# Loading expert matrices whole, 2 MB in seven buffers, instead of in halves in fourteen

## Chip, core and metric

The kernel runs on one core of one Trainium2 chip. The metric is device time in microseconds for one execution. A core has TensorE (PE, with its weight loads as PEld), VectorE (DVE), ScalarE (ACT), GpSimd (POOL) and SyncE (SP), and 16 DMA engines that carry out the transfers that SP, ACT and POOL issue.

## What is computed

One decoder layer on 512 tokens of width 1024, in float32. A combined projection feeds two attention branches, their gated outputs are merged and added to `x`, then comes a mixture of experts with 4 groups of 8, then a gated per-layer embedding and a final norm. The expert part, cut to what matters:

```python
D_MODEL = 1024; SEQ = 512; N_EXPERTS = 32; EXPERT_TOPK = 2; D_EXPERT = 512
expert_id = g[:, None] * EXPERTS_PER_GROUP + top_idx      # two experts of one group per token
def block_fn(args):                                       # for the rows of one expert
    tok_b, e_b = args
    xb = h_pad[tok_b]
    hid = jax.nn.silu(jnp.matmul(xb, w_gate[e_b])) * jnp.matmul(xb, w_up[e_b])
    return jnp.matmul(hid, w_down[e_b])
# w_gate, w_up: (32, 1024, 512); w_down: (32, 512, 1024); every matrix is 2 MB of float32
```

The weighted results are added back to the token rows.

## The kernel before

The program is written out by hand for each engine, with semaphores between them. Up to the routing (the front) its weights come in halves of 8 KB per partition into the ring `raw`, are split by ACT and DVE into two parts `w_hi` and `w_lo`, and multiplied. When the attention is done, ACT writes the normed rows to `h2_rows` in DRAM (profile name `h_rows`, line 1130), POOL gathers for each expert up to 64 of its rows into `xg` (three buffers, line 1545), PE turns them (line 854) and DVE scales them into `xt`.

The expert loop goes over 32 experts. `gate_up(e)` multiplies the rows by gate and up, eight k-tiles of 128 rows each (lines 878 and 879, side by side in the two halves of the array's columns; the trace shows two matmuls for each in the code); ACT and DVE make the hidden rows of it (lines 1143 and 1471); PE turns them (line 859, into `ht`, line 1487), and `down(e)` multiplies them, four k-tiles (lines 894 and 895). ACT weighs the result into `y` (line 1149), and POOL scatters it to `pair_rows` in DRAM (line 1550). PE's order is `gate_up(e + 1)`, the turn of the rows of `e + 2`, the turn of the hidden rows of `e`, `down(e)`.

All expert weights come through SP's queue (line 579), in the order of their use: `EXPERT_HALVES` lists gate and up of expert 0, then for each e gate and up of `e + 1` and down of `e`, every matrix cut into two halves: 128 partitions with 8 KB in a row, taken from rows that are 16 KB long in DRAM. A half holds four of the eight k-tiles of gate or up, or two of the four of down. There are 192 halves and fourteen buffers of 1 MB (`SLOTS`), which lie over memory of the front that comes free: `qk` when the branch products are done, the four `raw` buffers one by one as the splits (`lo_done`) go on, `w_hi`, `w_lo` and half of `act_hi` after the last `out` product, and one over `act_lo` after `h2_rows` is written (`h2_out`). From the fifteenth load on, SP waits for `half_used`, which PE raises when it is done with a half:

```python
        for n, (what, e, h) in enumerate(EXPERT_HALVES):
            if n >= SLOTS:
                sp.wait_ge(half_used, n - SLOTS + 1)
```

PE waits for each half by the semaphore of its buffer (`slot_loaded`). SP waits in order: a load whose wait isn't met holds back all behind it. Behind the experts stand six loads of the tail (`tail_raw`, line 532: two of `ple_proj` with 512 KB, four of `ple_gate` with 1 MB), also into expert buffers (`TAIL_RAW`), each behind the last use of its buffer, and then the loads of the summed pairs `y_in_even` and `y_in_odd` (line 600), which wait for the last scatter. A branch for experts with more than 64 rows (`over`) has loads of its own at line 591; the trace holds none of them.

Of the kernel before, what the change touches and what calls it, by code (L numbers as in the profile page):

```python
# [8 lines left out]
F32 = mybir.dt.float32  # L9
# [26 lines left out]
AHEAD = 2  # L36
SLOTS = 14
FIRST = 64
# [184 lines left out]

EXPERT_HALVES = expert_halves()
PLACE = {h: n for n, h in enumerate(EXPERT_HALVES)}
N_EXP = len(EXPERT_HALVES)
SLOT_REGION = [("qk", 0), ("qk", 1)] + [("raw", (N_FRONT - RAW + k) % RAW) for k in range(RAW)]
SLOT_REGION += [("whi", k) for k in range(SPLIT)] + [("wlo", k) for k in range(SPLIT)] + [("hi", 0), ("lo", 0)]
assert len(SLOT_REGION) == SLOTS
# [3 lines left out]
OVER_SLOTS = TAIL_HI + TAIL_LO  # L233
assert N_TAIL == 6 and N_EXP % SLOTS == 10

# [9 lines left out]
def layer_kernel(nc, x, p, g_attn, w_in, w_br_a, w_br_b, w_out, g_ffn, w_grp, b_grp, w_rt, b_rt,  # L245
# [13 lines left out]
    def sb(name, region, shape, dt=F32, skip=0):  # L259
        return nc.alloc_sbuf_tensor_at(name, shape, dt, offset=start[region] + skip)  # L260
# [10 lines left out]
    def sem(name):  # L271
# [6 lines left out]

    slot = [sb(f"slot_{k}", r, [P, HALF_W], skip=8 * K * j) for k, (r, j) in enumerate(SLOT_REGION)]
    slot_at = lambda k: start[SLOT_REGION[k][0]] + 8 * K * SLOT_REGION[k][1]  # L280
    tail_raw = [nc.alloc_sbuf_tensor_at(f"tail_raw_{m}", [P, HALF_W // (2 if m < 2 else 1)], F32, offset=slot_at(k) + skip)
                for m, (k, skip) in enumerate(TAIL_RAW)]
    tail_hi, tail_lo = ([nc.alloc_sbuf_tensor_at(f"tail_{n}_{j}", [P, HALF_W], F32R, offset=slot_at(k))
                         for j, k in enumerate(at)] for n, at in (("hi", TAIL_HI), ("lo", TAIL_LO)))
    raw_at = [raw[:, n % RAW, :] for n in range(N_FRONT)] + [v[:] for v in tail_raw]
# [29 lines left out]
    y_over = sb("y_over", "stage", [P, D], skip=4 * K)[:]  # L315
    xt = sb("xt", "hi", [P, 2, KD, FIRST], skip=8 * K)[:]
    xt_over = sb("xt_over", "hi", [P, KD, P], skip=12 * K)[:]
    ht = sb("ht", "lo", [P, FE // P, FIRST], skip=8 * K)[:]
    ht_over = sb("ht_over", "lo", [P, FE // P, P], skip=10 * K)[:]
    y_in = [nc.alloc_sbuf_tensor_at("y_in_even", [P, 2 * D], F32, offset=slot_at(Y_SLOT))[:],  # L320
            sb("y_in_odd", "small", [P, 2 * D])[:]]
# [155 lines left out]
    def split_high(act, n):  # L477
        if n < N_FRONT:
            act.wait_ge(raw_loaded[n % RAW], 16 * (n // RAW + 1))
            if n >= SPLIT:  # L480
                act.wait_ge(half_started, n - SPLIT + 2)
        else:
            m = n - N_FRONT
            act.wait_ge(tail_loaded[m], 16)
            if m < SPLIT:
                act.wait_ge(half_used, max(last_in_slot(TAIL_HI[m]), last_in_slot(TAIL_LO[m])) + 1)
# [11 lines left out]
    def split_next(s):  # L498
        n = HALF_OF[s] + AHEAD
        return n if n < (N_FRONT if HALF_OF[s] < N_FRONT else N_FRONT + N_TAIL) else None  # L500

    OVER_HALVES = [(what, h) for what in ("gate", "up", "down") for h in range(2)]
# [15 lines left out]
    def _(sp):  # L518
# [42 lines left out]

        def half_source(what, e, h):
            return views[what][e][:, h * HALF_W:(h + 1) * HALF_W]

        for n, (what, e, h) in enumerate(EXPERT_HALVES):
            if n >= SLOTS:
                sp.wait_ge(half_used, n - SLOTS + 1)
            elif SLOT_REGION[n][0] == "qk":
                for t in range(NT):
                    filled(sp, ("branch_b", 1, "tile", t))  # L570
            elif SLOT_REGION[n][0] == "raw":
                sp.wait_ge(lo_done, N_FRONT - RAW + n - 2 + 1)
            elif SLOT_REGION[n][0] in ("whi", "wlo"):
                filled(sp, ("out", 1, "tile", NT - 1))
            elif SLOT_REGION[n][0] == "hi":
# [8 lines left out]
        with sp.If(n_over > 0):  # L584
            with sp.Fori(0, NOVER) as i:
                with sp.If(i < n_over):
                    sp.wait_ge(half_used, N_EXP)
                    code = sp.value_load(over[0:1, bass.ds(i, 1)], min_val=0, max_val=NE * CH - 1)
                    e = sp.snap(code // CH, min_val=0, max_val=NE - 1)
                    for r, (what, h) in enumerate(OVER_HALVES):  # L590
                        sp.dma_start(slot[OVER_SLOTS[r]][:], half_source(what, e, h)).then_inc(ov_loaded[r], 16)
# [17 lines left out]
    def _(pe):  # L609
# [251 lines left out]

        def weights(slot_n, k):
            return slot[slot_n][:].rearrange("p (k n) -> p k n", k=k)

        def loaded(e, what, h):
            n = PLACE[what, e, h]
            pe.wait_ge(slot_loaded[n % SLOTS], 16 * (n // SLOTS + 1))
            return n % SLOTS

        def gate_up(e):  # L870
            ps = bank[2 + e % 2]
            pe.wait_ge(xt_done, e + 1)
            for h in range(2):
                g, u = (weights(loaded(e, what, h), 4) for what in ("gate", "up"))
                for k in range(4):
                    left = xt[:, e % 2, 4 * h + k, :]
                    first, last = h == 0 and k == 0, h == 1 and k == 3
                    mm_g = pe.matmul(ps[FIRST:2 * FIRST, :], left, g[:, k, :], start=first, stop=last)  # L878
                    mm_u = pe.matmul(ps[0:FIRST, :], left, u[:, k, :], start=first, stop=last)  # L879
                mm_g.then_inc(half_used, 1)  # L880
                mm_u.then_inc(half_used, 1)
            pe.sem_inc(pe_steps, 1)
            return mm_u

        def down(e):
            ps = bank[5 + e % 2]
            if e >= 2:
                pe.wait_ge(y_done, e - 1)
            for h in range(2):
                w = weights(loaded(e, "down", h), 2)  # L890
                for k in range(2):
                    first, last = h == 0 and k == 0, h == 1 and k == 1
                    left = ht[:, 2 * h + k, :]
                    pe.matmul(ps[0:FIRST, :], left, w[:, k, 0:512], start=first, stop=last)  # L894
                    mm = pe.matmul(ps[FIRST:2 * FIRST, :], left, w[:, k, 512:1024], start=first, stop=last)  # L895
                mm.then_inc(half_used, 1)

# [22 lines left out]
        with pe.If(n_over > 0):  # L920
            with pe.Fori(0, NOVER) as i:
                with pe.If(i < n_over):
# [4 lines left out]
                    for r, (what, h) in enumerate(OVER_HALVES[0:4]):  # L927
                        pe.wait_ge(ov_loaded[r], 16 * i + 16)
                        w = weights(OVER_SLOTS[r], 4)
# [8 lines left out]
                    for h in range(2):  # L938
                        pe.wait_ge(ov_loaded[4 + h], 16 * i + 16)
                        w = weights(OVER_SLOTS[4 + h], 2)  # L940
                        for k in range(2):
# [11 lines left out]
    def _(act):  # L953
# [185 lines left out]
        def silu(e):  # L1139
            act.wait_ge(half_used, PLACE["up", e, 1] + 1)  # L1140
            if e:
# [3 lines left out]
        def weigh(e):  # L1145
            act.wait_ge(half_used, PLACE["down", e, 1] + 1)
            if e >= 2:
# [475 lines left out]
```

## Time and profile before

| | us |
|---|---|
| median of 3 runs (1171.70 to 1173.94) | 1172.04 |
| the profiled execution | 1171.84 |
| its span, from the first to the last instruction | 1170.1 |

| engine | busy us | share of the span |
|---|---|---|
| PE | 980.4 | 84% |
| PEld | 613.8 | 52% |
| DVE | 371.6 | 32% |
| ACT | 277.4 | 24% |
| POOL | 95.5 | 8% |

The core read 258.38 MB from memory, of which the expert matrices are 201 MB. The shares are averages over stages with different limits, so each stage has to be read by itself. A chain of waits follows the work that ended last back to what released it. The duration of a DMA in it is the time from issue to landing, which for a queued transfer is mostly the time of those ahead of it. A DMA queue's row gives its packets, its bytes and the time that its packets took as a share of 16 engines over the stretch asked for. The granted clock of PE is 1.00 at 2.4 GHz and 0.50 at 1.2 GHz.

### The profile page before, as it was taken

How to read it: one execution, taken by the hardware profiler on the slowest of the kernel's cores; microseconds unless marked ns; L12 is line 12 of the kernel's file. 1: busy time of each engine (PE TensorE's matmuls, PEld its weight loads, DVE VectorE, ACT ScalarE, POOL GpSimd, SP SyncE). 2: the span in 40 equal slices, each digit the busy share in tenths (PEclk: the TensorE clock that was granted, in tenths of full speed). 3: DMA queues.
4: the chain of work that ended last, by engine and by line, in shares of the span. 5: the costliest groups of instructions: out<-in, count | busy, mean ns of one | idle time of the engine just before them, and what ended most of it. 6: DMA issues, size and time to landing. Idle time of an engine off the chain costs nothing.

```text
span 1170.1 us, 12032 instructions
## 1 busy us (share of the span) xinstructions
PE 980.4 (84%) x4656; PEld 613.8 (52%) x4656; DVE 371.6 (32%) x839; ACT 277.4 (24%) x487; POOL 95.5 (8%) x107
## 2 busy tenths in 40 slices
PE   3999999999989999995599987777877777777394
PEld 2765887777678888785233333233322333234383
DVE  6225597634643423314111110111101110012834
ACT  5234333444432222233001100000000000002513
POOL 0201202000000000000111111110111101100000
PEclk8999999999999999996699999999999999999697
DMA  8321232011033221608599999999999999998201
GB/s 278 116 101 36 79 107 72 2 37 37 1 127 108 77 104 36 234 1 323 196 358 397 405 401 404 414 403 403 410 400 413 401 402 401 406 417 332 91 1 72
DMA packets 59993, 263.39 MB, mean 225 GB/s; under 512 B 11662, under 2 KB 12302, under 8 KB 34848
## 3 DMA queue, kind: packets, MB, share of 16 engines
q1 hardware_dynamic: 49344, 248.26, 54.5%
q0 software_dynamic: 5120, 8.40, 2.2%
q10 hardware_dynamic: 5472, 5.94, 1.5%
q8 instruction: 38, 0.62, 0.2%
q14 instruction: 19, 0.16, 0.0%
HBM read 258.38 MB, written 12.58 MB: 232 GB/s over the span
## 4 chain that ended last, share of the span: by engine, by line
PE 56%; DMA 33%; DVE 6%; ACT 3%; issue 1%; SPq 1%; POOL 0%; ACTq 0%; POOLq 0%; DVEq 0%
PE psum L625 33%; DMA slot<-in_w_up 30%; PE psum L878 5%; PE psum L770 4%; PE psum L613 3%; PE psum L879 3%; PE psum L619 3%; PE psum L894 2%; DMA h_rows<-h_scaled 1%; DVE rows_tok L1204 1%; DVE act_lo L1240 1%; PE psum L759 1%; DMA y_in_odd<-pair_rows 1%; PE psum L854 1%; SPq L579 1%
## 5 line engine op out<-in xcount | busy, mean ns | idle before, releaser
L878 PE MATMUL psum<-slot,xt 128*64 128x512 f32 x512 | 239.1, 614 | 73.3 <-DMA slot<-in_w_up 72.5
L879 PE MATMUL psum<-slot,xt 128*64 128x512 f32 x512 | 240.4, 617 | 0.0
L878 PEld LDWEIGHTS psum<-slot,xt 128*64 128x64 f32 x512 | 68.1, 141 | 202.8 <-issue 201.8
L625 PE MATMUL psum<-w_hi,act_hi 128*128 128x512 f32 x416 | 165.0, 397 | 6.2 <-DVE act_lo L1240 3.7
L625 PE MATMUL psum<-w_hi,act_lo 128*128 128x512 f32 x416 | 163.5, 393 | 0.0
L625 PE MATMUL psum<-w_lo,act_hi 128*128 128x512 f32 x416 | 163.5, 393 | 0.0
L1476 DVE TENSOR_TENSOR xt<-psum,g_by_place 128x512 f32<-128x512 f32 x32 | 22.1, 692 | 436.3 <-PE psum L854 436.3
L894 PE MATMUL psum<-slot,ht 128*64 128x512 f32 x256 | 116.7, 598 | 20.0 <-DVE ht L1487 20.0
L895 PE MATMUL psum<-slot,ht 128*64 128x512 f32 x256 | 116.7, 598 | 0.0
L495 DVE TENSOR_TENSOR w_lo<-raw,w_hi 128x2048 fp32r<-128x2048 f32 (+1 forms) x31 | 70.0, 2260 | 132.3 <-ACT w_hi L490 132.3
L1143 ACT ACTIVATE small<-psum 64x512 f32<-64x512 f32 x32 | 19.0, 595 | 318.5 <-PE psum L879 281.2
L625 PEld LDWEIGHTS psum<-w_hi,act_hi 128*128 128x128 f32 x416 | 79.1, 190 | 25.6 <-issue 9.5
L625 PEld LDWEIGHTS psum<-w_lo,act_hi 128*128 128x128 f32 x416 | 79.0, 190 | 16.8
L625 PEld LDWEIGHTS psum<-w_hi,act_lo 128*128 128x128 f32 x416 | 79.0, 190 | 16.0
L879 PEld LDWEIGHTS psum<-slot,xt 128*64 128x64 f32 x512 | 68.1, 141 | 27.4 <-issue 27.4
L490 ACT CAST w_hi<-raw 128x2048 fp32r<-128x2048 f32 (+1 forms) x31 | 57.8, 1869 | 96.8 <-PE psum L625 96.5
L894 PEld LDWEIGHTS psum<-slot,ht 128*64 128x64 f32 x256 | 32.4, 136 | 79.2 <-issue 54.8
L1550 POOL DMA_INDIRECT pair_rows<-y,slot_pair x32 | 32.4, 1012 | 435.7 <-ACT y L1149 435.7
L1149 ACT ACTIVATE y<-psum,slot_weight 128x512 f32<-128x512 f32 x32 | 22.0, 687 | 164.1 <-PE psum L895 164.1
L1059 ACT ACTIVATE small<-small,nm 128x128 f32<-128x128 f32 (+1 forms) x64 | 36.0, 562 | 72.8 <-DVE nm L1263 62.4
L770 PE MATMUL psum<-kt,qt 64*128 64x128 f32 (+3 forms) x128 | 50.9, 480 | 0.0
L854 PEld LDWEIGHTS psum<-cst,xg 64*128 64x128 f32 x256 | 30.6, 200 | 35.2 <-issue 25.1
(219 smaller groups left out, 1189.2 us busy)
## 6 DMA issues: line engine op xcount, KB each, us to landing
slot<-in_w_gate SPq DMA_DIRECT2D x64, 1024.0 KB, 29.1
slot<-in_w_up SPq DMA_DIRECT2D x64, 1024.0 KB, 29.2
slot<-in_w_down SPq DMA_DIRECT2D x64, 1024.0 KB, 29.4
raw<-in_w_in SPq DMA_DIRECT2D x22, 1024.0 KB, 5.0
raw<-in_w_out SPq DMA_DIRECT2D x4, 1024.0 KB, 5.1
tail_raw<-in_w_ple_gate SPq DMA_DIRECT2D x4, 1024.0 KB, 15.0
rows_tok<-in_x SPq DMA_DIRECT2D x4, 512.0 KB, 6.5
raw<-in_w_br_a SPq DMA_DIRECT2D x2, 1024.0 KB, 5.2
```

The lines of the kernel that those rows point to most:

```text
L490: act.copy(w_hi_at[n][:, 0:w], raw_at[n][:, 0:w]).then_inc(hi_done, 1)
L495: dve.tensor_tensor(w_lo_at[n][:, 0:w], raw_at[n][:, 0:w], w_hi_at[n][:, 0:w].bitcast(F32), ALU.subtract).then_inc(lo_done, 1)
L613: mm = pe.transpose(ps[0:v.shape[1], n * P:(n + 1) * P], v, ident)
L619: mm = pe.matmul(ps, a, b, start=(n == 0), stop=(n == len(pairs) - 1))
L625: mms = [pe.matmul(ps, a, b, start=first and n == 0, stop=last and n == 2) for n, (a, b) in enumerate(ops)]
L770: pe.matmul(ps[:, 0:(t + 1) * P], qt[lo:lo + HD, h // 2, t * P:(t + 1) * P], kt_[lo:lo + HD, h // 2, 0:(t + 1) * P], start=True, stop=True ...
L854: mm = pe.transpose(x_turns(n_rows)[:, k, :], rows[:, k:D:KD], ident[0:n_rows, 0:n_rows])
L878: mm_g = pe.matmul(ps[FIRST:2 * FIRST, :], left, g[:, k, :], start=first, stop=last)
L879: mm_u = pe.matmul(ps[0:FIRST, :], left, u[:, k, :], start=first, stop=last)
L894: pe.matmul(ps[0:FIRST, :], left, w[:, k, 0:512], start=first, stop=last)
L895: mm = pe.matmul(ps[FIRST:2 * FIRST, :], left, w[:, k, 512:1024], start=first, stop=last)
L1059: act.activation(small[:, 2 + i % 2, 0:(t + 1) * P], small[:, i % 2, 0:(t + 1) * P], ACT.Exp, bias=nm[:, i % 4:i % 4 + 1], scale=-1.0, acc ...
```

## The change

Each expert matrix is loaded by one transfer, 128 partitions with 16 KB in a row, into one of seven buffers of 2 MB that lie over nearly the same memory. Their number in bytes is the same. The list of loads has 96 entries instead of 192. PE waits for gate and up whole before the first k-tile, raises `half_used` once for each matrix, and so SP may refill a buffer only when the whole matrix is used. The two buffers over `raw` both wait for the last split; the one over half of `act_hi` and half of `act_lo` waits for `h2_out`. `xt` moves within `act_hi`. The tail's loads and its `tail_hi` and `tail_lo` get other buffers: the first two tail loads now lie in the buffer of up of expert 31, the next two in that of down of 29, the last two in that of down of 30. The loads of the `over` branch still come in halves.

```diff
-SLOTS = 14
+SLOTS = 7
...
-def expert_halves():
-
-    gate_up = lambda e: [("gate", e, 0), ("up", e, 0), ("gate", e, 1), ("up", e, 1)]
-    down = lambda e: [("down", e, 0), ("down", e, 1)]
+def expert_loads():
+
+    gate_up = lambda e: [("gate", e), ("up", e)]
     out = gate_up(0)
     for e in range(NE):
         if e + 1 < NE:
             out += gate_up(e + 1)
-        out += down(e)
+        out.append(("down", e))
     return out
...
-SLOT_REGION = [("qk", 0), ("qk", 1)] + [("raw", (N_FRONT - RAW + k) % RAW) for k in range(RAW)]
-SLOT_REGION += [("whi", k) for k in range(SPLIT)] + [("wlo", k) for k in range(SPLIT)] + [("hi", 0), ("lo", 0)]
...
-TAIL_RAW = [(2, 0), (2, 4096)] + [(3 + k, 0) for k in range(4)]
-TAIL_HI, TAIL_LO = [10, 0, 8], [11, 1, 9]
-Y_SLOT = 7
...
+SLOT_AT = [("qk", 0), ("raw", 0), ("raw", 2 * K8), ("whi", 0), ("whi", 2 * K8), ("wlo", K8), ("hi", K8)]
...
+TAIL_RAW = [(2, 0), (2, 4096), (0, 0), (0, K8), (3, 0), (3, K8)]
+TAIL_HI, TAIL_LO = [(1, 0), (4, 0), (5, 0)], [(1, K8), (4, K8), (5, K8)]
+Y_SLOT = 2
...
-    xt = sb("xt", "hi", [P, 2, KD, FIRST], skip=8 * K)[:]
+    xt = sb("xt", "hi", [P, 2, KD, FIRST])[:]
...
-            elif SLOT_REGION[n][0] == "raw":
-                sp.wait_ge(lo_done, N_FRONT - RAW + n - 2 + 1)
...
+            elif region == "raw":
+                sp.wait_ge(lo_done, N_FRONT)
...
-            sp.dma_start(slot[n % SLOTS][:], half_source(what, e, h)).then_inc(slot_loaded[n % SLOTS], 16)
+            sp.dma_start(slot[n % SLOTS][:], views[what][e]).then_inc(slot_loaded[n % SLOTS], 16)
...
-            for h in range(2):
-                g, u = (weights(loaded(e, what, h), 4) for what in ("gate", "up"))
-                for k in range(4):
-                    left = xt[:, e % 2, 4 * h + k, :]
-                    first, last = h == 0 and k == 0, h == 1 and k == 3
-                    mm_g = pe.matmul(ps[FIRST:2 * FIRST, :], left, g[:, k, :], start=first, stop=last)
-                    mm_u = pe.matmul(ps[0:FIRST, :], left, u[:, k, :], start=first, stop=last)
-                mm_g.then_inc(half_used, 1)
-                mm_u.then_inc(half_used, 1)
+            g, u = (weights(loaded(what, e), KD) for what in ("gate", "up"))
+            for k in range(KD):
+                left = xt[:, e % 2, k, :]
+                mm_g = pe.matmul(ps[FIRST:2 * FIRST, :], left, g[:, k, :], start=k == 0, stop=k == KD - 1)
+                mm_u = pe.matmul(ps[0:FIRST, :], left, u[:, k, :], start=k == 0, stop=k == KD - 1)
+            mm_g.then_inc(half_used, 1)
+            mm_u.then_inc(half_used, 1)
```

On SP's queue, where the first expert loads stand (the numbers behind `slot_` are those of the program's tensors: 53 is the first buffer; `bank_filled_7` is the last `out` product), before:

```order
L579 DMA slot_57<-in_w_gate 128x2048 [waits lo_done]
L579 DMA slot_58<-in_w_up 128x2048 [waits lo_done]
L579 DMA slot_59<-in_w_gate 128x2048 [waits bank_filled_7]
L579 DMA slot_60<-in_w_up 128x2048 [waits bank_filled_7]
L579 DMA slot_61<-in_w_down 128x2048 [waits bank_filled_7]
L579 DMA slot_62<-in_w_down 128x2048 [waits bank_filled_7]
L579 DMA slot_63<-in_w_gate 128x2048 [waits bank_filled_7]
L579 DMA slot_64<-in_w_up 128x2048 [waits bank_filled_7]
L579 DMA slot_65<-in_w_gate 128x2048 [waits bank_filled_7]
L579 DMA slot_66<-in_w_up 128x2048 [waits h2_out]
L579 DMA slot_53<-in_w_down 128x2048 [waits half_used]
```

and after:

```order
L579 DMA slot_53<-in_w_gate 128x4096 [waits bank_filled_6,bank_filled_7,bank_filled_5,bank_filled_4]
L579 DMA slot_54<-in_w_up 128x4096 [waits lo_done]
L579 DMA slot_55<-in_w_gate 128x4096 [waits lo_done]
L579 DMA slot_56<-in_w_up 128x4096 [waits bank_filled_7]
L579 DMA slot_57<-in_w_down 128x4096 [waits bank_filled_7]
L579 DMA slot_58<-in_w_gate 128x4096 [waits bank_filled_7]
L579 DMA slot_59<-in_w_up 128x4096 [waits h2_out]
L579 DMA slot_53<-in_w_down 128x4096 [waits half_used]
```

Seven halves stand behind the last `out` product and one behind `h2_out` before; three wholes and one whole after.

On PE, at the middle of `gate_up(0)`, between the fourth and the fifth k-tile, before:

```order
L879 MATMUL psum<-slot_54,xt 64x512
L878 MATMUL psum<-slot_53,xt 64x512
L879 MATMUL psum<-slot_54,xt 64x512
L878 MATMUL psum<-slot_55,xt 64x512 [waits slot_loaded_3,slot_loaded_2]
L879 MATMUL psum<-slot_56,xt 64x512
```

and after, at its start:

```order
L876 MATMUL psum<-slot_53,xt 64x512 [waits slot_loaded_1,slot_loaded_0,xt_done]
L877 MATMUL psum<-slot_54,xt 64x512
L876 MATMUL psum<-slot_53,xt 64x512
L877 MATMUL psum<-slot_54,xt 64x512
L876 MATMUL psum<-slot_53,xt 64x512
```

The wait in the middle is gone; the wait at the start is now for the whole of both matrices. PE has the same number of matmuls, in the same order.

## Rows read from the trace of the kernel before

**Rows 1.** The page, the span in 40 slices of 29.25 us: GB/s
```profile
GB/s 278 116 101 36 79 107 72 2 37 37 1 127 108 77 104 36 234 1 323 196 358 397 405 401 404 414 403 403 410 400 413 401 402 401 406 417 332 91 1 72
```

**Rows 2.** Windows: us, busy of PE, PEld, DVE, ACT, POOL, PEclk, DMA share, GB/s
```profile
600.00:640.00 40.00, 38.10 (x192) 14.96 (x188) 4.83 (x9) 3.84 (x6) 5.93 (x6) 1.00 1.02 402
640.00:740.00 100.00, 83.05 (x402) 33.61 (x400) 11.26 (x21) 8.97 (x14) 13.81 (x14) 0.98 1.02 404
```

**Rows 3.** The chain in order of time, PE's turns of `xg`: start us, us, what
```profile
589.88 1.04 PE psum L854 x8
...
602.54 1.04 PE psum L854 x8
```

**Rows 4.** DMA queues from 640 to 1040 us: packets, MB, share of 16 engines
```profile
q1 hardware_dynamic: 21323, 155.27, 96.3%
```

**Rows 5.** Waits: engine line, waited for: us in total, times, longest us
```profile
PE psum L878 <- DMA slot<-in_w_up: 72.5, 45, 2.3
```

**Rows 6.** Timeline of SP's queue, the fourteenth load and those into freed buffers: start us, us, what
```profile
555.99 0.33 SPq L579 DMA_DIRECT2D slot<-in_w_up  x1
571.58 0.80 SPq L579 DMA_DIRECT2D slot<-in_w_down  x2
575.02 0.33 SPq L579 DMA_DIRECT2D slot<-in_w_gate  x1
...
586.47 0.33 SPq L579 DMA_DIRECT2D slot<-in_w_gate  x1
...
589.91 0.91 SPq L579 DMA_DIRECT2D slot<-in_w_down  x2
594.00 0.33 SPq L579 DMA_DIRECT2D slot<-in_w_gate  x1
```

**Rows 7.** The chain in order of time, between the front and the experts
```profile
539.97 16.01 DMA h_rows<-h_scaled
556.85 6.33 DMA xg<-h_rows,slot_token
```

**Rows 8.** DMA queues from 471 to 487 us, four to five loads in a row
```profile
q1 hardware_dynamic: 714, 5.19, 80.8%
```

**Rows 9.** Transfers into `xg`, from issue to landing
```profile
DMA to landing us min/median/max: 2.9/7.6/8.7
```

**Rows 10.** DMA queues from 491 to 498 us, one expert load alone
```profile
q1 hardware_dynamic: 144, 1.05, 43.1%
```

**Rows 11.** DMA queues from 30 to 60 us, loads of 2 KB rows
```profile
q1 hardware_dynamic: 1993, 3.98, 39.4%
```

**Rows 12.** DMA queues from 338 to 349 us, `x_after` on q10
```profile
q10 hardware_dynamic: 528, 2.10, 53.1%
```

**Rows 13.** The chain in order of time, from the last expert loads on
```profile
1022.69 31.03 DMA slot<-in_w_up
...
1053.86 0.61 PE psum L878
...
1057.51 0.64 PE psum L859 x4
...
1067.14 0.70 ACT y L1149
...
1068.60 5.60 DMA pair_rows<-y,slot_pair
```

**Rows 14.** Timeline of SP's queue, the first tail loads
```profile
1052.57 0.89 SPq L532 DMA_DIRECT2D tail_raw<-in_w_ple_proj  x2
```

**Rows 15.** Timeline of PE in `gate_up(1)`: start us, us, what
```profile
581.27 1.11 PE L878 MATMUL psum<-slot,xt 128*64 128x512 f32 x1
...
584.99 0.59 PE L878 MATMUL psum<-slot,xt 128*64 128x512 f32 x1
...
585.42 0.59 PE L878 MATMUL psum<-slot,xt 128*64 128x512 f32 x1
```

**Rows 16.** Window from 578 to 582 us, columns as in rows 2
```profile
578.00:582.00 4.00, 1.49 (x8) 0.93 (x10) 2.57 (x13) 0.00 (x0) 0.00 (x0) 0.50 1.02 430
```

More of the change, by code:

```diff
@@ L219, in expert_halves @@
             out += gate_up(e + 1)
[L220 removed]
+        out.append(("down", e))
     return out
[L224 to L234 removed]
+EXPERT_LOADS = expert_loads()
+PLACE = {h: n for n, h in enumerate(EXPERT_LOADS)}
+N_EXP = len(EXPERT_LOADS)
+K8 = 8 * 1024
+SLOT_AT = [("qk", 0), ("raw", 0), ("raw", 2 * K8), ("whi", 0), ("whi", 2 * K8), ("wlo", K8), ("hi", K8)]
+assert len(SLOT_AT) == SLOTS and SPLIT == 3 and RAW == 4
+TAIL_RAW = [(2, 0), (2, 4096), (0, 0), (0, K8), (3, 0), (3, K8)]
+TAIL_HI, TAIL_LO = [(1, 0), (4, 0), (5, 0)], [(1, K8), (4, K8), (5, K8)]
+Y_SLOT = 2
+OVER_AT = [(1, 0), (1, K8), (4, 0), (4, K8), (5, 0), (5, K8)]
+assert N_TAIL == 6
 X1_TURNS = [("first", 0), ("first", 1), ("first", 2), ("second", 0), ("first", 3), ("second", 1), ("second", 2),
@@ L277, in layer_kernel @@
     w_lo = sb("w_lo", "wlo", [P, SPLIT, HALF_W], F32R)
-    slot = [sb(f"slot_{k}", r, [P, HALF_W], skip=8 * K * j) for k, (r, j) in enumerate(SLOT_REGION)]
-    slot_at = lambda k: start[SLOT_REGION[k][0]] + 8 * K * SLOT_REGION[k][1]
+    slot = [sb(f"slot_{k}", r, [P, 2 * HALF_W], skip=skip) for k, (r, skip) in enumerate(SLOT_AT)]
+    slot_at = lambda k: start[SLOT_AT[k][0]] + SLOT_AT[k][1]
     tail_raw = [nc.alloc_sbuf_tensor_at(f"tail_raw_{m}", [P, HALF_W // (2 if m < 2 else 1)], F32, offset=slot_at(k) + skip)
                 for m, (k, skip) in enumerate(TAIL_RAW)]
-    tail_hi, tail_lo = ([nc.alloc_sbuf_tensor_at(f"tail_{n}_{j}", [P, HALF_W], F32R, offset=slot_at(k))
-                         for j, k in enumerate(at)] for n, at in (("hi", TAIL_HI), ("lo", TAIL_LO)))
+    tail_hi, tail_lo = ([nc.alloc_sbuf_tensor_at(f"tail_{n}_{j}", [P, HALF_W], F32R, offset=slot_at(k) + skip)
+                         for j, (k, skip) in enumerate(at)] for n, at in (("hi", TAIL_HI), ("lo", TAIL_LO)))
     raw_at = [raw[:, n % RAW, :] for n in range(N_FRONT)] + [v[:] for v in tail_raw]
@@ L315, in layer_kernel @@
     y_over = sb("y_over", "stage", [P, D], skip=4 * K)[:]
[L316 to L317 removed]
+    xt = sb("xt", "hi", [P, 2, KD, FIRST])[:]
+    xt_over = sb("xt_over", "hi", [P, KD, P], skip=4 * K)[:]
     ht = sb("ht", "lo", [P, FE // P, FIRST], skip=8 * K)[:]
     ht_over = sb("ht_over", "lo", [P, FE // P, P], skip=10 * K)[:]
[L320 removed]
+    y_in = [nc.alloc_sbuf_tensor_at("y_in_even", [P, 2 * D], F32, offset=slot_at(Y_SLOT) + K8)[:],
             sb("y_in_odd", "small", [P, 2 * D])[:]]
@@ L500, in split_next, with over_slot @@
         return n if n < (N_FRONT if HALF_OF[s] < N_FRONT else N_FRONT + N_TAIL) else None
+    def over_slot(r):
+        k, skip = OVER_AT[r]
+        return slot[k][:, skip // 4:skip // 4 + HALF_W]
     OVER_HALVES = [(what, h) for what in ("gate", "up", "down") for h in range(2)]
@@ L560, in _ @@
                  "down": w_down[0].rearrange("e (p k) d -> e p (k d)", p=P)}
-        def half_source(what, e, h):
-            return views[what][e][:, h * HALF_W:(h + 1) * HALF_W]
-        for n, (what, e, h) in enumerate(EXPERT_HALVES):
+        for n, (what, e) in enumerate(EXPERT_LOADS):
+            region = SLOT_AT[n % SLOTS][0]
             if n >= SLOTS:
                 sp.wait_ge(half_used, n - SLOTS + 1)
-            elif SLOT_REGION[n][0] == "qk":
+            elif region == "qk":
                 for t in range(NT):
                     filled(sp, ("branch_b", 1, "tile", t))
-            elif SLOT_REGION[n][0] == "raw":
-                sp.wait_ge(lo_done, N_FRONT - RAW + n - 2 + 1)
-            elif SLOT_REGION[n][0] in ("whi", "wlo"):
-                filled(sp, ("out", 1, "tile", NT - 1))
-            elif SLOT_REGION[n][0] == "hi":
+            elif region == "raw":
+                sp.wait_ge(lo_done, N_FRONT)
+            elif region in ("whi", "wlo"):
                 filled(sp, ("out", 1, "tile", NT - 1))
@@ L590, in _ @@
                     for r, (what, h) in enumerate(OVER_HALVES):
-                        sp.dma_start(slot[OVER_SLOTS[r]][:], half_source(what, e, h)).then_inc(ov_loaded[r], 16)
+                        sp.dma_start(over_slot(r), views[what][e][:, h * HALF_W:(h + 1) * HALF_W]).then_inc(ov_loaded[r], 16)
                     sp.wait_ge(ov["scattered_0"], 16 * i + 16)
@@ L860, in turn_hidden, with weights, loaded @@
             mm.then_inc(done, 1)
[L862 to L866, printed above, removed]
+        def weights(v, k):
+            return v.rearrange("p (k n) -> p k n", k=k)
+        def loaded(what, e):
+            n = PLACE[what, e]
             pe.wait_ge(slot_loaded[n % SLOTS], 16 * (n // SLOTS + 1))
-            return n % SLOTS
+            return slot[n % SLOTS][:]
         def gate_up(e):
@@ L888, in down @@
                 pe.wait_ge(y_done, e - 1)
[L889 to L896, printed above, removed]
+            w = weights(loaded("down", e), FE // P)
+            for k in range(FE // P):
+                first, last = k == 0, k == FE // P - 1
+                pe.matmul(ps[0:FIRST, :], ht[:, k, :], w[:, k, 0:512], start=first, stop=last)
+                mm = pe.matmul(ps[FIRST:2 * FIRST, :], ht[:, k, :], w[:, k, 512:1024], start=first, stop=last)
+            mm.then_inc(half_used, 1)
         def turn_x(e):
@@ L1145, in weigh @@
         def weigh(e):
-            act.wait_ge(half_used, PLACE["down", e, 1] + 1)
+            act.wait_ge(half_used, PLACE["down", e] + 1)
             if e >= 2:
```

8 lines of the change are left out of this document (4 added, 4 removed).

## The prediction

> **What bounds the kernel now.** I read the slices of the span first [rows 1]. From about 585 to 1053 us the core's DMA engines move some 400 GB/s in every slice and nowhere else for so long; this is the expert stage, which loads 201 MB. The stages by windows [rows 2] say the same: from 600 to 740 us the mean DMA share is 1.02 (packets overlap, so full) at 402 to 404 GB/s, while PE is busy 38 of 40 us at first and 83 of 100 later. So there are two parts. Until about 650 us PE sets the pace: it begins a new expert every 12.66 us by the chain (589.88 to 602.54) [rows 3]. After that DMA does: between 640 and 1040 us queue q1 moved 155.27 MB, which is 148.1 loads of 1.0486 MB, so 2.70 us a load and 16.2 us for the six loads of an expert [rows 4]. PE needs 12.66 of those, and what it waits for is `slot<-in_w_up`, 72.5 us in all [rows 5]. The stage's end is therefore the time at which the load stream became unbroken, plus what was left to load by the pace of the stream, plus what PE does after the last loads land. The change touches all three.
>
> **The stream's start.** Fourteen halves, 14.7 MB, fit before and seven wholes, the same bytes, fit after; they are loaded before the first expert product in both. Then a buffer must come free. SP issues the next loads at 571.58 and 575.02, then at 586.47 and 589.91 us [rows 6]: each pair of halves is free 3.4 us before the next pair, since a product over four k-tiles of gate and up takes that long (575.02 - 571.58). The four halves issued from 571.6 to 575.4, at 2.6 us each, are moved by about 584, so DMA then stands still until 586.47 and is unbroken from there. After the change nothing is free until the whole product is done: both whole matrices of expert 0 are issued at the place of 575.02 and those of expert 1 at the place of 589.91. In both kernels 18 halves (or 9 wholes) are issued before that point, so the unbroken stream starts **3.4 us later**. It does not break again: 4.2 MB last 10.4 us, and the next buffer (down of expert 0) is free some 6 us later, where the two halves of it are now issued (594.00 is its first half) [rows 6].
>
> Two things ahead of that move too. Of the last loads before the experts, seven halves are issued when the last `out` product is done and one at 555.99 [rows 6], after `h_rows` is written. Now it is three wholes (six halves) and one whole. The write of `h_rows` is the chain's piece from 539.97, 16.01 us long [rows 7], because its packets share the engines with those loads. One load less in front of it at 2.6 us (12.93 us for 4.96 loads, [rows 8]) is **-2.6 us**; it would be 0 if the writes got their turn among the loads anyway. Against it, the gather of the first expert's rows `xg` is next in the chain at 6.33 us [rows 7], and a gather with idle engines has landed in 2.9 [rows 9]; it now shares with a load of twice the size. Bounds 0 and +2.6 (one more half ahead of it); I take **+1.5**, since the gather's few packets need not wait for the whole of it.
>
> The two loads that go to the freed `raw` buffers wait for the last split of the front, which the load alone at 491 us had waited for too [rows 10], instead of one split after the other. The experts begin some 70 us later, so nothing.
>
> **The stream's pace.** 87 wholes instead of 174 halves are left. Per whole, each of 16 engines sees 8 data packets of 16 KB instead of 16 of 8 KB, and one completion packet instead of two. No row has a 16 KB packet. The nearest are these. One 8 KB-row load alone was busy 43.1% of 7 us, 3.02 us [rows 10]; in a stream 2.61 us [rows 8]. Loads of 2 KB rows (33 packets an engine instead of 9), mostly alone, took 39.4% of 30 us for 3.98 MB, 3.11 us each [rows 11]. The 24 packets more cost 0.09 us against the load that was alone too, 4 ns a packet, and 0.50 us against the stream, 21 ns. At 4 ns the 8 packets saved are 0.03 us a whole, **-2.7 us** in 87; at 21 ns 0.17 us, -15 us. On the other side, the only 2.1 MB transfer with one completion, `x_after` in 4 KB rows, was busy 53.1% of 11 us, 5.84 us [rows 12], where 3.02 + 2.61 = 5.63 would be one alone and one more in stream: 0.21 us worse, +18 us in 87. I take -2.7 because it compares like with like, and keep both ends. That fewer loads are outstanding costs nothing: at worst gate, up and one down are held and four wholes, over 20 us of work, are queued.
>
> The Trainium skill ("DMA: Bandwidth & Descriptors", Anatomy of one DMA) gives every DMA some 2.0 us of fixed cost and therefore favours fewer, larger ones. That would be an estimate of 87 x 2 = 174 us saved if queued transfers paid it; the loads queued in a row at 2.61 us each for 1.05 MB disagree, so it is not in the sum.
>
> **The end.** The last wait for a load is for up of expert 31: a load issued at 1022.69 lands 31.03 us later, the first product follows at 1053.86, next transposes at 1057.51, then down of 30, transposes, down of 31, and `y` at 1067.14 [rows 13]. After the change all eight k-tiles wait for that landing, not four: **+3.4 us**, and nothing hides it, since the down loads land 5 and 10 us later and PE reaches them after 8 and 13. After it come the scatter at 1068.60, and the two `y_in` loads, all waiting for that `y`, so they move with it. SP also issues the six tail loads later: at 1052.57 now [rows 14], since the first wants one half of gate 31, and after the change when up of 31 is used, some 8 us later. The bytes ahead of them are still moving then (10 us of down loads from 1053.7), and the `y_in` loads come at 1078, so I cost it at nothing; if it failed it would be some 2 us.
>
> **The clock.** PE's waits for a load, 45 of them with 1.6 us in the mean and 2.3 at most [rows 5] and mostly two an expert, become one of some 3.5 us (16.2 - 12.66). After the pause before 581.27 a matmul took 1.11 us, and later ones took 0.59 and stood 0.43 apart [rows 15]: the granted clock was 0.50 up to 582 us, the level of 1.2 GHz [rows 16], and then that of 2.4. About four pairs at the slow level are 4 x 0.43 = 1.7 us. Within the stream PE has 3.5 us to spare, so this costs only in the last product: 0 to +1.7, I take **+0.9**.
>
> Sum: +3.4 - 2.6 + 1.5 - 2.7 + 3.4 + 0.9 = **+3.9 us**. The profiled execution took 1171.84 us (span 1170.1 and 1.7 around it), which is 0.2 below the median of 1172.04. Forecast 1175.7 us. The terms without the stream's pace reach from 3.4 - 2.6 + 0 + 3.4 + 0 = +4.2 to 3.4 + 0 + 2.6 + 3.4 + 1.7 = +11.1.
>
> **Rivals.** *Packets count for more (faster).* If a packet costs the 21 ns of the stream comparison, the sum is +6.6 - 15 = -8: 1163.4 us. For it: the steady stream of 2.70 us a load is slower than four loads in a row at 2.61. Against it: the 2 KB loads were not in a long stream. It wins as soon as a whole load saves over 0.08 us of 5.2. The Trainium skill ("DMA: Bandwidth & Descriptors", Where 436 GB/s comes from) puts the ceiling at 435 GB/s, an estimate of 2.41 us per half; that would allow at most 174 x 0.2, some 35 us, and no run here shows that pace over a whole stage.
>
> *Large transfers run worse (slower).* At 0.21 us a whole as `x_after` had it, +6.6 + 18 = +25: 1196.4 us. For it only that one row, with 4 KB rows and other traffic beside it; it decides from 0.1 us on.
>
> *The rows stay cut.* If a 16 KB row travels as two packets of 8 KB, the change does not do what it says on the wire; only the coarser release is left, +6.6: 1178.4 us. For it: every 1.05 MB half shows 144 packets, 128 rows and 16 completions, and nothing larger than 8 KB occurs in the trace, so it is untested. Against it: 2, 4 and 8 KB rows each are one packet.
>
> **Chances.** Forecast (pace within some 4 us of -2.7) 0.56, packets count 0.24, worse transfers 0.08, cut rows 0.12. Within the forecast a quarter lies inside 0.2%, which is about what a measurement of this kernel can tell from no change (2.3 us). So faster 0.24, same 0.20, slower 0.56. The range 1163 to 1183 takes in the packet rival at its price and the upper bounds of the small terms, and leaves out the worse transfers and a yet larger gain.
>
> **What would show it.** Right: q1 packets in the stage halve; SP's first issue for a freed buffer near 575, the next near 589, each with two wholes; the write of `h_rows` about 13.5 us; `y` of expert 31 some 17 us after up 31 lands instead of 13.4; a pace near 5.37 us per whole from 640 to 1040 us. Wrong: a pace below 5.30 or above 5.47 us, 256 + 16 packets a whole, or pauses of the stream after 650 us.

## The result and the profile after

The changed kernel is slower: 1178.95 us in the median of seven runs against 1173.94 in nine of the kernel before. Two more runs of it, at some 1218 us, fell into a slower state with a lower granted clock, which the kernel before shows too (at some 1212 to 1215 us), and such runs are left out of all times and ratios here. The ratio is 1.0045, 95% interval 1.0029 to 1.0061, so +3.4 to +7.2 us. The forecast was +3.9 us. A second comparison (e0_after, below) gave 1.0058 (1.0043 to 1.0073). The profiled execution took 1180.57 us, with a span of 1178.8.

The whole span by slices of 29.5 us, GB/s, answers to [rows 1]:

```profile
GB/s 276 111 102 39 72 91 93 1 1 72 1 110 88 107 107 36 121 112 286 191 325 403 409 405 408 406 401 410 413 415 405 408 408 411 404 409 294 115 1 71
```

The stage is still bound by DMA. Its queues from 640 to 1040 us (packets, MB, share of 16 engines) answer to [rows 4]:

```profile
q1 hardware_dynamic: 10738, 156.39, 95.8%
```

Half the packets (21323 before) carry a little more: a matrix of 2.097 MB takes 5.364 us in place of 5.403 (400 us over the matrices moved in them). So a row of 16 KB does travel as one packet: 128 rows and 16 completions for each of the 74.6 matrices are these 10738. The issues of SP (start us, us, what), to be laid beside [rows 6]:

```profile
559.49 0.33 SPq L579 DMA_DIRECT2D slot<-in_w_up  x1
580.66 0.33 SPq L579 DMA_DIRECT2D slot<-in_w_down  x1
581.03 0.43 SPq L579 DMA_DIRECT2D slot<-in_w_gate  x1
596.75 0.33 SPq L579 DMA_DIRECT2D slot<-in_w_up  x1
597.12 0.43 SPq L579 DMA_DIRECT2D slot<-in_w_down  x1
602.56 0.33 SPq L579 DMA_DIRECT2D slot<-in_w_gate  x1
```

Before there were two steps for each of the first products, 3.4 us apart; now there is one, at its end. They come later than the 575 and 589 that the prediction named, at 580.7 and 596.8; some 5.8 us of both is that the last `h_rows` issue itself came later (545.72 against 539.97). The chain in order of time (start us, us, what), for [rows 7] and [rows 13]:

```profile
545.72 13.75 DMA h_rows<-h_scaled
...
560.35 9.38 DMA xg<-h_rows,slot_token
...
1038.10 22.98 DMA slot<-in_w_up
...
1061.21 0.61 PE psum L876
...
1077.93 0.70 ACT y L1145
...
1079.39 6.05 DMA pair_rows<-y,slot_pair
...
1085.52 4.78 DMA y_in_even<-pair_rows
```

These pieces join into an account of everything from the last issue for `h_rows` to the end. I took it for two profiles of either kernel: the one before and e8_before, the one after and e0_after.

| us | before | e8_before | after | e0_after |
|---|---|---|---|---|
| write of `h_rows` | 16.01 | 15.97 | 13.75 | 13.61 |
| up to the gather's issue | 0.87 | 0.88 | 0.88 | 0.88 |
| gather of the first `xg` | 6.33 | 5.48 | 9.38 | 9.19 |
| up to the refill from which the stream is unbroken | 23.29 | 22.94 | 27.02 | 27.19 |
| from there to the landing of up 31 | 467.25 | 466.96 | 464.33 | 464.88 |
| from there to `y` of expert 31 | 13.42 | 13.42 | 16.85 | 16.85 |
| to the end of the span | 102.96 | 101.78 | 100.87 | 100.75 |
| sum | 630.13 | 627.43 | 633.08 | 633.35 |

On average the sum grows by 4.4 us; the two profiles of the kernel before differ by 2.7 among themselves, so this is good to a microsecond or so. The span of the profile after is 8.7 longer than that of the profile before: 2.95 of it lie in the table, and 5.75 ahead of it, in the front, where nothing is changed. Two windows of the profile after (us, busy of PE, PEld, DVE, ACT, POOL, PEclk, DMA share, GB/s) show what it is:

```profile
60.00:90.00 30.00, 27.08 (x114) 20.26 (x114) 8.16 (x10) 9.21 (x20) 1.91 (x6) 0.83 0.27 90
90.00:120.00 30.00, 28.17 (x95) 16.25 (x94) 14.31 (x17) 11.54 (x20) 5.40 (x6) 0.91 0.11 36
```

The granted clock of PE was 0.83 and 0.91 there; in the profile before it was 1.00.

### The profile page after: what moved, and what is told of

The parts are those of the page before. It is cut to its first block, busy times and chain, and to the rows that moved or that the text cites. A ratio compares the mean times of both kernels' runs of the same rounds, so it can differ in the third digit from the quotient of the medians.

```text
span 1178.8 us, 11902 instructions
## 1 busy us (share of the span) xinstructions
PE 1004.4 (85%) x4656; PEld 626.0 (53%) x4656; DVE 371.4 (32%) x839; ACT 277.1 (24%) x487; POOL 95.3 (8%) x107
## 4 chain that ended last, share of the span: by engine, by line
PE 60%; DMA 30%; DVE 6%; ACT 2%; issue 1%; POOL 0%; ACTq 0%; SPq 0%; POOLq 0%; DVEq 0%
PE psum L625 33%; DMA slot<-in_w_up 26%; PE psum L876 10%; PE psum L770 4%; PE psum L613 3%; PE psum L877 3%; PE psum L619 3%; PE psum L890 2%; DMA h_rows<-h_scaled 1%; PE psum L759 1%; DVE rows_tok L1200 1%; DVE act_lo L1236 1%; DMA xg<-h_rows,slot_token 1%; DMA rows_tok<-in_x 1%; PE psum L854 1%
## 5 line engine op out<-in xcount | busy, mean ns | idle before, releaser
L876 PE MATMUL psum<-slot,xt 128*64 128x512 f32 x512 | 254.9, 656 | 62.3 <-DMA slot<-in_w_up 61.5
L877 PE MATMUL psum<-slot,xt 128*64 128x512 f32 x512 | 255.5, 657 | 0.0
L876 PEld LDWEIGHTS psum<-slot,xt 128*64 128x64 f32 x512 | 74.7, 151 | 208.9 <-issue 207.9
L625 PEld LDWEIGHTS psum<-w_hi,act_hi 128*128 128x128 f32 x416 | 79.7, 192 | 26.8 <-issue 10.5
L877 PEld LDWEIGHTS psum<-slot,xt 128*64 128x64 f32 x512 | 74.8, 151 | 18.3 <-issue 18.3
```

The source lines that it names most:

```text
L625: mms = [pe.matmul(ps, a, b, start=first and n == 0, stop=last and n == 2) for n, (a, b) in enumerate(ops)]
L877: mm_u = pe.matmul(ps[0:FIRST, :], left, u[:, k, :], start=k == 0, stop=k == KD - 1)
```

## The experiments

All kernels ran in five rounds beside the kernel before on the same chip; ratios are to that kernel. e0, e1, e2 and e3 shared one chip, e4 to e7 another, e8 to e11 a third. e1 to e7 and e9 are written with two semaphores for each buffer, so that either form of loading fits in; where they load whole, they issue what the changed kernel issues. Kernels of two chips are compared by their ratios, each of which has its own interval.

| kernel | ratio | 95% interval |
|---|---|---|
| e0_after | 1.0058 | 1.0043 to 1.0073 |
| e3_coarse_both | 1.0052 | 1.0037 to 1.0066 |
| e2_coarse_release | 1.0028 | 1.0016 to 1.0040 |
| e1_halves_fine | 0.9999 | 0.9987 to 1.0011 |
| e4_last_split | 1.0038 | 1.0024 to 1.0051 |
| e5_first_split | 1.0007 | 0.9994 to 1.0020 |
| e6_both_ends | 0.9996 | 0.9981 to 1.0010 |
| e7_both_ends_hold | 0.9939 | 0.9922 to 0.9956 |
| e8_before | 0.9995 | 0.9982 to 1.0008 |
| e9_hold_two | 0.9912 | 0.9898 to 0.9926 |
| e10_halves_hold | 0.9927 | 0.9915 to 0.9939 |
| e11_hold_last | 1.0000 | 0.9989 to 1.0012 |

**e0_after**, the changed kernel beside the next three.

> The changed kernel again, beside the others of this chip. Theory: the loss is +3.4 us at the first refill (a buffer comes free only when the whole matrix is used), +3.4 us after the last load lands, and a gain of 3 to 4 us in the stream's pace, with some +3 us from the slower gather of the first rows. So +4 to +7 us against the kernel before, as first measured (ratio 1.0045).

1.0058, so +5.0 to +8.6 us. The interval overlaps the first one.

**Down the ladder: one coarse step after the other undone, in the layout of the changed kernel.** First the size of the transfers alone, e3_coarse_both:

```diff
-            sp.dma_start(slot[n % SLOTS][:], views[what][e]).then_inc(slot_loaded[n % SLOTS], 16)
+            if h is not None:
+                sp.dma_start(slot[n % SLOTS][:, h * HALF_W:(h + 1) * HALF_W], views[what][e][:, h * HALF_W:(h + 1) * HALF_W]
+                             ).then_inc((second_loaded if h else slot_loaded)[n % SLOTS], 16)
+                continue
```

> The seven buffers and all waits as in the changed kernel, but each matrix comes as two transfers of 1 MB with 8 KB rows, one behind the other. It isolates the size of transfer and packet. Theory (a saved packet is worth some 4 ns): pace 5.40 us per 2.1 MB instead of 5.36, so +3 to +4 us against the changed kernel. Rival (packet size and number of transfers cost nothing, the faster pace of one profile was scatter): 0 +- 1 us, pace 5.36. If the 16 KB packets are what slows the first gather, the piece xg in the chain is back from 9.4 to some 6 to 8 us and the total is +1 only.

The queue from 640 to 1040 us:

```profile
q1 hardware_dynamic: 21355, 155.51, 96.4%
```

5.394 us for each matrix, against 5.365 in e0_after: 0.03 us, and 0.03 x 87 is the 2.6 us that the prediction gave to the packets. The time, for which +3 to +4 us were expected, doesn't show it: 1.0052 against 1.0058, whose difference, -0.7 us, has intervals of some 1.8 us on both sides. In the trace the stretch from the unbroken refill to the landing of up 31 is 465.92 us, 1.0 more than e0_after has. So the pace is a property that all kernels with whole loads in the stream share (5.352 to 5.376 in eight profiles; 5.390 to 5.404 in six with halves), but a loss of 2.6 us by smaller transfers was not seen end to end.

The first gather is 8.98 us here, 8.69 in e2 and 8.28 in e1, all with two halves ahead of it, and 9.18 to 9.51 in the five profiles with one whole load ahead. So most of its length comes from the 2.1 MB ahead of it, and how they are cut makes some 0.7 us on average. Within the stream it is otherwise. All transfers into `xg`, e0_after and then e3_coarse_both, whose loads stand in the same order:

```profile
DMA to landing us min/median/max: 3.0/10.4/11.8
```

```profile
DMA to landing us min/median/max: 3.0/7.8/9.0
```

The median is 10.2 to 10.5 us in the eight profiles with whole loads and 7.6 to 7.8 in the six with halves, while the loads queued ahead there take 23 to 31 us to land. So a gather in the stream does not wait for all that is queued, and what it waits for grows with the transfer or its rows. It costs nothing there: PE waits for a gather only once, for the first.

Next the wait at the product's start undone as well, e2_coarse_release: halves of gate and up take turns, PE waits for each.

> Seven buffers refilled only when a whole matrix is used, loads in halves of 8 KB rows, halves of gate and up taking turns, PE waits for each half by itself. It takes the late start of the last product away and leaves the late first refill. Theory: 3.4 us less than with both coarse waits. Rival (the end is hidden by the tail's own loads): no difference to that one. From the last load of up landing to y of the last expert some 13.4 us instead of 16.9.

1.0028, 0.24% or 2.8 us less than with both coarse. The chain's pieces from the landing of up (1031.79 + 27.27 = 1059.06) to `y`:

```profile
1031.79 27.27 DMA slot<-in_w_up
...
1072.48 0.70 ACT y L1181
...
1073.94 5.92 DMA pair_rows<-y,slot_pair
...
1080.34 8.62 DMA y_in_odd<-pair_rows
```

13.42 us, as in [rows 13], against 16.85 with the coarse wait: 3.43 us to the digit. Behind `y` some of it is given back: the chain now goes through `y_in_odd`, 8.62 us from issue to landing as in [rows 13]'s run, where the coarse kernels have `y_in_even` and 4.7 to 5.0, and 103.4 us are left from `y` to the end, against 100.8 to 101.0.

Then the refill by halves too, e1_halves_fine (against e2 its one difference is the `True`, which is `False` there):

```diff
-                sp.wait_ge(half_used, n - SLOTS + 1)
+                sp.wait_ge(half_used, half_at(n - SLOTS, h if h is not None and True else 1))
```

> Halves in every respect (loads, refills, waits) but in the memory layout and order of the changed kernel, with three matrices and not seven halves ahead of the write of h_rows. Theory: another 3.4 us less than with the coarse refill alone, so the time of the kernel before or 0 to 3 us below it (h_rows sooner by 2.3 us). Rival (the layout, or the tail loads that now wait for up of expert 31, cost the time): it stays 3 us or more above the kernel before.

0.9999: another 0.29%, 3.4 us, and level with the kernel before. The two coarse waits together are 6.2 us of the 6.8; the layout and the tail loads behind expert 31 cost nothing that shows.

**The same from the other side: whole loads except at the ends.** e4_last_split splits gate and up of expert 31 alone:

```diff
+SPLIT_LOADS = {PLACE["gate", NE - 1], PLACE["up", NE - 1]}
```

> The changed kernel, but gate and up of expert 31 alone come in halves that take turns, each waited for by itself. Theory: 3.4 us less than the changed kernel: y of the last expert 13.4 us after the last half of up lands instead of 16.9, all else alike. Rival (the tail loads hide it): under 1 us.

1.0038. Against the 1.0045 and the 1.0058 of the changed kernel, from other comparisons, that is 0.8 to 2.3 us less, with intervals of some 2 us. The trace shows the mechanism up to `y`: from the unbroken refill to `y` of expert 31 it takes 478.5 us, where the two profiles of the changed kernel take 481.2 and 481.7, and PE no longer stops for up 31 at all; its last wait for a load is that for up of expert 30. Behind `y` 0.9 us are lost again (101.7 us to the end against 100.8). The full 3.4 us do not show in the time. e5_first_split splits the first four refills:

```diff
+SPLIT_LOADS = {SLOTS, SLOTS + 1, SLOTS + 2, SLOTS + 3}
```

> The changed kernel, but the first four loads into freed buffers come in halves, each issued when its half is free. Theory: the unbroken stream starts some 3.4 us sooner and the time is 3.4 us less than the changed kernel's. Rival (the stream is not what ends last, or its start is set by the clock of the first products): under 1 us.

1.0007: 4.5 to 6.0 us less than the changed kernel, more than the 3.4 expected. Its issues:

```profile
576.88 0.33 SPq L607 DMA_DIRECT2D slot<-in_w_down  x1
577.25 0.43 SPq L607 DMA_DIRECT2D slot<-in_w_gate  x1
580.31 0.33 SPq L607 DMA_DIRECT2D slot<-in_w_down  x1
580.69 0.43 SPq L607 DMA_DIRECT2D slot<-in_w_gate  x1
592.92 0.33 SPq L607 DMA_DIRECT2D slot<-in_w_up  x1
```

Counted from the last `h_rows` issue the unbroken stream begins at 47.66 us here, at 50.38 in e4_last_split, 50.87 in e0_after, so 2.7 to 3.2 us sooner, which is the mechanism at its price. Why the time fell by more I can't say; its ten runs reach from 1171.8 to 1179.3, the widest of all these kernels. The profiled execution was the slowest of them, and part of that is the clock, which was down when the product of expert 30 began:

```profile
1044.00:1048.00 4.00, 4.00 (x10) 1.07 (x9) 0.00 (x0) 0.00 (x0) 0.00 (x0) 0.50 1.01 428
```

Six pairs of its matmuls stand 0.85 us apart instead of 0.43, which is 2.6 us.

Both together, e6_both_ends:

> Both of these edits: halves for the first four refills and for gate and up of expert 31, whole matrices of 16 KB rows in between. Theory: the terms add up, 6.9 us less than the changed kernel, so 0 to 3 us below the kernel before (the pace of whole loads stays). Rival: the terms overlap, and it stays at or above the kernel before.

0.9996, 0.42% (4.9 us) less than e4 on the same chip and 1.3 us less than e5; against the changed kernel 5.8 to 7.3 us, where 6.9 were expected. The end's 3.4 us shows again at under half its size in e6 against e5. So whole loads with fine ends are level with the kernel before, not below it by more than the interval.

**The gather.** e11_hold_last is the changed kernel with its seventh load behind the first gather:

```diff
+            if n == 6:
+                sp.wait_ge(gathered[0], 16)
```

> The changed kernel with one edit: the seventh load (up of expert 2) waits until the first gather has landed instead of for h_rows alone. It prices the gather beside a 2.1 MB load, which was put at +1.5 us and looks like +3. Theory: the chain's piece xg falls from 9.2 to 9.5 us to some 3 to 5, everything to the first refill comes 4 to 6 us sooner, and the time falls by 4 to 5 us against the changed kernel. Rival (the gather is long because of its own cold start, not the load beside it): the piece stays above 8 us and the time the same.

Its chain:

```profile
542.66 13.58 DMA h_rows<-h_scaled
...
557.12 2.95 DMA xg<-h_rows,slot_token
```

The gather is 6.2 to 6.4 us shorter, and the ratio falls from 1.0045 and 1.0058 to 1.0000, 5.3 to 6.8 us, where 4 to 5 were expected. With this one line the changed kernel is level with the kernel before. The transfer in front, not a cold start, made the gather long.

**The engines left to the small transfers.** e7_both_ends_hold holds down 0, gate 2 and up 2 until that gather has landed:

```diff
+            if n == 4 and h in (None, 0): sp.wait_ge(gathered[0], 16)
```

> As both ends, and the last three of the seven loads ahead of the experts (down 0, gate 2, up 2) are held back on SP until the first gather of rows has landed, so that the write of h_rows and the gather have the DMA engines nearly to themselves. Theory: h_rows takes some 4 to 6 us instead of 13.8 and the gather some 3 to 5 instead of 9.4, the experts begin 6 us or more sooner (then the slot lists bound them, at about 550 us in the kernel before), the stream is unbroken from there, and the time is 6 to 12 us below both ends alone. Rival: the three loads come so late that the first products or the stream wait for them, and nothing is gained.

0.9939, 6.7 us below e6, at the low end of the 6 to 12 expected. The gathers of POOL (idle before, releaser in brackets):

```profile
550.02 1.12 POOL L1577 DMA_INDIRECT xg<-h_rows,slot_token  x1 [7.52 <-DVE slot_token L1434]
```

What they wait for now is `slot_token`, the list of slots made by DVE, no longer `h_rows`: the write is off the path. The windows from there show what was left:

```profile
545.00:550.00 5.00, 3.64 (x16) 3.48 (x16) 1.64 (x9) 0.22 (x1) 0.00 (x0) 0.50 0.01 3
550.00:555.00 5.00, 4.36 (x23) 4.30 (x24) 1.08 (x4) 0.00 (x0) 3.01 (x3) 0.50 0.47 96
```

3 GB/s for five microseconds. e9_hold_two gives that time to down 0 and holds two loads:

```diff
-            if n == 4 and h in (None, 0): sp.wait_ge(gathered[0], 16)
+            if n == 5 and h in (None, 0): sp.wait_ge(gathered[0], 16)
```

> As both ends with the hold, but down 0 goes ahead of the held loads too, so that only gate 2 and up 2 wait for the first gather. In the run with three held the DMA engines stood still from 545 to 553 us and h_rows was written long before the slot lists were ready at 550. Theory: that pause takes one more 2.1 MB load, h_rows ends by 550 still, the stream starts with 5 us less to do: 4 to 5 us below the kernel with three held, so about 1161. Rival (h_rows ends later and the experts with it): no gain.

0.9912, a median of 1163.76 us: 8.7 to 12.0 us below the kernel before and the fastest of all, by 3.2 below e7 where 4 to 5 were expected. The gather's wait shows where the rest went:

```profile
554.81 1.15 POOL L1577 DMA_INDIRECT xg<-h_rows,slot_token  x1 [7.95 <-DMA h_rows<-h_scaled]
```

It is `h_rows` again, 9.5 us after its last issue at 545.31, where in e7 the lists were ready 9.1 us after it: the two are nearly level. Is it the whole matrices that make this? e10_halves_hold is the kernel before with its last four halves held:

```diff
+            if n == 10:
+                sp.wait_ge(gathered[0], 16)
```

> The kernel before with its fourteen halves, and its last four loads ahead of the experts (the eleventh to the fourteenth) held back until the first gather has landed: the same bytes ahead as with two wholes held. Theory: the hold is worth the same with halves, some 11 to 13 us, and whole matrices add only the 2.7 us of the pace: 1161 to 1164, 0 to 3 us above the two held wholes. Rival (the gain needs the larger transfers): under half of it.

0.9927, 1164.94 us. The hold is worth 7.2 to 10.0 us with halves as well, less than the 11 to 13 I expected, and whole matrices with fine ends add 0.15%, 1.8 us, which the intervals don't separate.

**e8_before** was run for its profile.

> The kernel before, once more with a profile. All nine profiles of the seven-buffer kernels have a granted clock of 0.83 to 0.89 somewhere between 60 and 120 us, where nothing is changed, and the one profile of the kernel before has 1.00; their first expert load is issued 2.4 to 7.4 us later. Theory (chance): this profile too shows a dip there in some executions, and its first expert load is issued at 470 to 475 us. Rival (the shorter program moves something in the front): again 1.00 and 470. Ratio 1.000 +- 0.001.

0.9995. Its windows over the front:

```profile
60.00:90.00 30.00, 27.25 (x118) 20.69 (x117) 6.81 (x10) 10.00 (x20) 1.91 (x6) 0.89 0.22 71
90.00:120.00 30.00, 28.01 (x104) 17.27 (x103) 16.91 (x18) 13.03 (x20) 5.40 (x6) 1.00 0.11 36
```

A dip of the clock here too, and the first expert load issued at 472.15 us instead of 469.92. So the dip is not of the change's making. But the first expert load comes at 472.0 us on average in the three profiles with fourteen buffers (469.9 to 473.8) and at 474.6 in the eleven with seven (472.3 to 477.3). Six of the eleven make up 1.6 us of it on the way: at the last `h_rows` issue, where the table above begins, the averages are 542.0 and 543.8. Whether these 1.8 us are chance or a shift that the other program brings stays open.

## Why the prediction was right, point by point

The direction, the mechanism and the range (1163 to 1183) held; the size was short by one to three microseconds. That it came so near is in part luck, since terms that were off by up to 1.9 us cancelled (below).

- **Refill only when the whole matrix is used, +3.4.** Right. From the landing of the first gather to the unbroken stream it is 4.0 us more (27.1 against 23.1), of which some 0.6 is the clock in the first two products (10 and 11 steps of 0.85 us between their pairs of matmuls, against 9 in either profile before); undoing it gave 3.4 us in the ladder (e1 against e2), with an interval of some 2 us.
- **One load less ahead of `h_rows`, -2.6.** Right: 2.3 us (15.99 to 13.68).
- **The gather beside a load of twice the size, +1.5 with bounds of 0 and +2.6.** This is the term that was mis-sized: +3.4 us (5.9 to 9.3). I assumed that the gather's few packets would not wait for the whole load, and took one more half as the upper bound. The gather alone is 2.95 us (e11), with 1 MB in front 5.5 to 6.3, with 2.1 MB 9.2 to 9.5: each megabyte in front is worth its full time and some more, so this gather does wait for all of that one load. (The gathers in the stream, above, show that this is no rule for everything queued.) The row for this was in the trace: 6.33 against a least landing of 2.9 [rows 7, 9] is 3.4 us for 1 MB, and I should have added 3.4 again.
- **Pace of the stream, -2.7.** Right in the trace: 5.364 and 5.365 us for each matrix where 5.37 was named, and 2.5 us less over the whole stretch; but e3, with the same waits and smaller transfers, gives back only 1.0 of this in the stretch and nothing in the time, so that the transfers' size is worth 2.7 us end to end is not shown. A matrix also saves nine packets on each engine (144 of 288 in all), not the eight of the sum, which forgot the completion; that is 0.3 us in 87. The comparison of like with like, 4 ns for each packet, held in the pace, and neither the 21 ns of the stream comparison nor the 0.21 us of `x_after` showed up. Both rivals on the pace fell, and so did that of cut rows (10738 packets). The 2.0 us of fixed cost, kept out of the sum, is given by the Trainium skill ("DMA: Bandwidth & Descriptors", Anatomy of one DMA) for DMAs issued by GpSimd. These loads are issued by SP, and one transfer less for each matrix saved 0.03 to 0.04 us in the pace.
- **The last product waits for all of up 31, +3.4.** Right up to `y` (16.85 against 13.42), but 1.6 us of it came back behind it (100.8 against 102.4 us to the end), since the `y_in` loads landed sooner after their issue. "All waiting for that `y`, so they move with it" was too strong. What makes them land sooner was not tried.
- **Clock, +0.9.** It didn't come in the two profiles of the changed kernel: the last product ran at 0.43 us a pair from its first. In e11_hold_last, whose end is the same, it did. The last product began at 1050.98 us, and the window from there shows a granted clock of 0.65:

```profile
1050.00:1054.00 4.00, 3.02 (x8) 1.12 (x10) 0.00 (x0) 0.00 (x0) 0.99 (x1) 0.65 0.75 318
```

  From the landing of up 31 to `y` it took 18.55 us there instead of 16.85, which is the term's upper bound of 1.7. Of the four profiles whose last product waits for up 31 whole (these three and e3) one shows it, so the term's bounds were right and its middle was high. The clock did fall more often in the stream (0.95, 0.91, 0.95 and 0.93 in its four windows of 100 us against [rows 2]'s 0.98), where PE has time to spare.

The mis-sized gather adds 1.9 us to the forecast, the give-back and the missing clock take 2.5 off, the clock in the first products adds 0.6, and the write and the pace, each a little short, add 0.5: with 4.4 us the account is near the forecast by terms that cancel. The runs have 1 to 2.4 us on top (5.3 and 6.8 by their ratios). The front, 1.8 us later on average, is about as much, and is the open point above.

Two sums of the prediction do not come out, though nothing hung on them. The chances: with a quarter of the forecast's 0.56 inside 0.2%, and both slower rivals beside it, "same" would have 0.14 and "slower" 0.62, not 0.20 and 0.56. And the 35 us that a pace of 2.41 us a load would save start from 2.61; from the stream's own 2.70 the same estimate gives some 50.

## What to carry to other kernels

When a stage is bound by a stream of loads, the size of a load matters at its two ends: how soon the first buffer can be refilled, and how much work waits for the last landing. Load large in the middle if it is convenient (it was worth 0.5 to 0.7% of the pace in the traces, and nothing that the times of e3 or e10 could separate), and split the first refills and the last matrix. And look at what small transfers stand on the path beside the bulk: here one wait on the issuing queue, which held four megabytes back until a gather had landed, was worth more than every change of size, because those loads had some 30 us to spare (in the profile after, the first product that reads one of them, `down(0)`, begins at 598.86, 29 us behind the gather's landing) and the gather had none.

## What the runs showed of the hardware

A gather of 64 rows that was issued 0.9 us behind a bulk load, with no other load queued, waited for that load: 2.95 us with none ahead, 5.5 to 6.3 behind 1 MB, 9.2 to 9.5 behind 2.1 MB in one transfer of 16 KB rows, 8.3 to 9.0 behind the same bytes in two of 8 KB rows. In the full stream, with 23 to 31 us of loads queued, it landed after 7.6 to 7.8 us in the median beside 8 KB rows and after 10.2 to 10.5 beside 16 KB rows.

In the kernel before an issue of an expert load held SP for 2.1 to 2.2 us in the median; with whole matrices it held it for 0.33 to 0.43. The rows of the two kernels, all loads of `down` (min/median/max ns):

```profile
L579 SPq DMA_DIRECT2D slot<-in_w_down x64: 327/2132/6458, 530.6 to 1036.7; - x64
```

```profile
L579 SPq DMA_DIRECT2D slot<-in_w_down x32: 327/432/434, 535.9 to 1043.9; - x32
```

In both cases a load in the stream landed some 23 to 31 us after its issue, so about as many bytes were queued, by an estimate from the paces about eleven halves against about five wholes. It is not halves as such that hold SP: in e3_coarse_both, also with halves, the medians are 0.38 to 0.49 us, and its loads landed after 22.9 to 28.4 us in the median, so some nine to ten were queued. That it is the number of queued transfers fits both, but no run tried it alone. Nothing depended on it here.
